# Down weights of the experts loaded as whole 16 KB rows, with the inner features interleaved to match

## The reference, cut to what matters

```
D_MODEL = 1024; N_EXPERTS = 32; D_EXPERT = 512; TOP_K_FINE = 2

def expert_block(args):
    xblk, e = args
    hid = jax.nn.silu(xblk @ w_gate[e]) * (xblk @ w_up[e])
    return hid @ w_down[e]
```

## Time and profile before

| What | Value |
|---|---|
| Time, median of 3 runs | 2542.81 us (2533.68 to 2543.42) |
| Time of the profiled execution | 2544.94 us |
| Span in its profile | 2543.2 us |
| PE matmul busy | 2271.7 us, 89% of the span |
| PE weight load busy | 1283.3 us |
| DVE, ACT, POOL busy | 825.4, 489.2, 308.4 us |
| Bytes moved by DMA | 536.48 MB |
| Loads of gate, up, down matrices | 64 each, 2048 KB each |

### The profile page before, as it was taken

The page is one execution under the profiler, slowest core; times in us unless marked ns, Lnnn a source line. Parts: engine busy times, 40 slices in busy tenths (PEclk is TensorE's granted clock), DMA queues, the critical chain, the costliest instruction groups (busy, mean ns, idle before and its releaser), DMA issues. The chain is left out here.

```text
span 2543.2 us, 33362 instructions
## 1 busy us (share of the span) xinstructions
PE 2271.7 (89%) x13415; PEld 1283.3 (50%) x13415; DVE 825.4 (32%) x1631; ACT 489.2 (19%) x894; POOL 308.4 (12%) x265
## 2 busy tenths in 40 slices
PE   6999977889958999999977999999976999999994
PEld 4687545554545445545534555554544545554541
DVE  5652125553241111111126455564323111111116
ACT  2222124341100000000013444442110010000002
POOL 5342000001101111110012000001000110110102
PEclk9999978789968999999988999999976999999997
DMA  4100010002129999999959110102108999999977
GB/s 147 35 34 1 17 68 1 1 1 71 66 100 401 420 412 405 410 412 416 415 225 301 41 37 26 30 27 61 58 25 335 417 411 409 407 405 421 400 287 282
DMA packets 144327, 536.48 MB, mean 211 GB/s; under 512 B 38370, under 2 KB 61442, under 8 KB 127792
## 3 DMA queue, kind: packets, MB, share of 16 engines
q1 hardware_dynamic: 122640, 490.93, 49.1%
q0 software_dynamic: 13600, 40.52, 4.2%
q10 hardware_dynamic: 7936, 2.90, 0.5%
HBM read 500.50 MB, written 40.50 MB: 213 GB/s over the span
## 5 line engine op out<-in xcount | busy, mean ns | idle before, releaser
L1729 PE MATMUL l_main_pgu<-l_w_ring,l_ex_xT 128*64 128x256 f32 (+1 forms) x4992 | 484.8, 383 | 2.4 <-DVE l_ex_xT L1804 1.8
L1729 PEld LDWEIGHTS l_main_pgu<-l_w_ring,l_ex_xT 128*64 128x64 f32 (+1 forms) x4992 | 292.6, 129 | 184.1 <-issue 39.7
L1775 PE MATMUL l_main_py<-l_w_ring,l_ex_hT 128*64 128x512 f32 (+1 forms) x1248 | 239.3, 595 | 1.6 <-DVE l_ex_hT L1843 1.6
L1726 PE MATMUL l_main_pgu<-l_w_ring,l_ex_xT 128*128 128x512 f32 x384 | 174.8, 610 | 15.2 <-DMA l_w_ring<-in_l_moe_w_gate 15.2
L1843 DVE COPY l_ex_hT<-l_main_ph 128x256 f32<-128x256 f32 (+1 forms) x78 | 36.3, 466 | 393.1 <-PE l_main_ph L1750 393.1
L2186 PE MATMUL lru_pr<-h2T,lru_wz 128*128 128x352 f32 (+1 forms) x480 | 144.1, 461 | 9.0 <-ACTq L2235 9.0
L1839 DVE TENSOR_TENSOR l_ex_hid<-l_ex_sil,l_main_pgu 128x256 f32<-128x256 f32 (+1 forms) x78 | 36.1, 462 | 351.2 <-PE l_main_pgu L1729 269.8
L1775 PEld LDWEIGHTS l_main_py<-l_w_ring,l_ex_hT 128*64 128x64 f32 (+1 forms) x1248 | 71.5, 128 | 136.6 <-issue 129.6
L2191 PE MATMUL lru_pg<-h2T,lru_wz 128*128 128x512 f32 x320 | 139.0, 592 | 0.0
L1726 PEld LDWEIGHTS l_main_pgu<-l_w_ring,l_ex_xT 128*128 128x128 f32 x384 | 73.2, 195 | 105.9 <-issue 87.8
L2186 PEld LDWEIGHTS lru_pr<-h2T,lru_wz 128*128 128x128 f32 x480 | 92.1, 193 | 59.4 <-ACTq L2235 9.4
(11 more groups left out here) (433 smaller groups left out, 2839.2 us busy)
## 6 DMA issues: line engine op xcount, KB each, us to landing
l_w_ring<-in_l_moe_w_gate SPq DMA_DIRECT2D x64, 2048.0 KB, 26.3
l_w_ring<-in_l_moe_w_up SPq DMA_DIRECT2D x64, 2048.0 KB, 27.4
l_w_ring<-in_l_moe_w_down SPq DMA_DIRECT2D x64, 2048.0 KB, 30.2
l_y<-expert_rows SPq DMA_DIRECT2D x32, 512.0 KB, 6.8
h_rows<-H SPq DMA_DIRECT2D x24, 512.0 KB, 5.2
lru_wz<-in_l_w_in SPq DMA_DIRECT2D x20, 512.0 KB, 4.9
H<-h_rows SPq DMA_DIRECT2D x16, 512.0 KB, 8.4
w_in<-in_l_w_in SPq DMA_DIRECT2D x3, 2048.0 KB, 8.0
```

The source lines that it names most:

```text
L1726: last = pe.matmul(out[:], x[:, k, :], w[0][:, k, :], start=k == 0, stop=k == KD - 1)
L1729: last = pe.matmul(out[HALF * h + o:HALF * h + o + m, 0:256], x[:, k, it.at + o:it.at + o + m], w[n][:, k, 256 * h:256 * h + 256], start=k ...
L1775: last = pe.matmul(py[b][HALF * h + o:HALF * h + o + m, :], hT[:, c % 2, HALF * (c // 2) + o:HALF * (c // 2) + o + m], ws[n][:, c, 512 * h ...
```

## The change

The down matrix is read as `e (p c) d -> e p (c d)`: partition p gets rows 4p to 4p+3, one piece of 16 KB. All three kinds of load now have one form. Chunk c of the down product then holds features 4p+c. To fit this,

- a big item's hidden columns are turned in steps of four (columns c, 4+c, 8+c and so on), where they were turned as a block of 128,
- in half and shared items, tile h streams of every four columns of the gate and up weights the pair 2h, 2h+1 (`half_features`), where it streamed 256 columns in a row; its hidden columns are turned in steps of two.

No instruction is added, removed or moved on any engine; the number of elements of each is the same. The products of big items (line 1726) and all down products stream what they streamed, columns in a row.

```
-    E.src["down"] = K.A[f"{L}_moe_w_down"].rearrange("e (c p) d -> e p c d", p=P)
+    E.src["down"] = K.A[f"{L}_moe_w_down"].rearrange("e (p c) d -> e p (c d)", p=P)
...
+def half_features(w, k, h):
+    return w[:, k, :].rearrange("r (p c) -> r p c", c=4)[:, :, 2 * h:2 * h + 2]
...
+def hidden_chunk(hid, c, chunks):
+    return hid[:, 0:P * chunks].rearrange("s (p c) -> s c p", c=chunks)[:, c, :]
...
 def load_unit(sp, E, unit, kind, e, sem):
-    if kind < DOWN:
-        sp.dma_start(E.ring[:, unit % UNITS, :], E.src[("gate", "up")[kind]][ds(e, 1)].rearrange("a p x -> (a p) x")).then_inc(sem, 16)
-    else:
-        sp.dma_start(down_view(E, unit), E.src["down"][ds(e, 1)].rearrange("a p c d -> (a p) c d")).then_inc(sem, 16)
+    sp.dma_start(E.ring[:, unit % UNITS, :], E.src[("gate", "up", "down")[kind]][ds(e, 1)].rearrange("a p x -> (a p) x")).then_inc(sem, 16)
...
-                            last = pe.matmul(out[HALF * h + o:HALF * h + o + m, 0:256], x[:, k, it.at + o:it.at + o + m], w[n][:, k, 256 * h:256 * h + 256],
+                            last = pe.matmul(out[HALF * h + o:HALF * h + o + m, 0:256], x[:, k, it.at + o:it.at + o + m], half_features(w[n], k, h),
...
-                for c in range(4 if items[i].big else 2):
-                    last = pe.transpose(ph[:, c, :], hid[i % 2][:, P * c:P * c + P], K.ident[:])
+                chunks = 4 if items[i].big else 2
+                for c in range(chunks):
+                    last = pe.transpose(ph[:, c, :], hidden_chunk(hid[i % 2], c, chunks), K.ident[:])
```

More of the change, by code:

```diff
@@ L1942, in step @@
                     for h in range(2):
-                        last = pe.matmul(out[HALF * h:HALF * h + HALF, 0:256], xT[par][:, k, 0:HALF], w[:, k, 256 * h:256 * h + 256], start=k == 0, stop=k == KD - 1)
+                        last = pe.matmul(out[HALF * h:HALF * h + HALF, 0:256], xT[par][:, k, 0:HALF], half_features(w, k, h), start=k == 0, stop=k == KD - 1)
                 last.then_inc(ready, 1)
@@ L1946, in step @@
             for c in range(2):
-                last = pe.transpose(ph[:, c, :], hid[par][:, P * c:P * c + P], K.ident[:])
+                last = pe.transpose(ph[:, c, :], hidden_chunk(hid[par], c, 2), K.ident[:])
             last.then_inc(self.h_turned, 1)
```

## The result

| | Before | After |
|---|---|---|
| Time, median (lowest to highest) | 2542.75 us (2533.68 to 2543.42, and one of 5448.15) | 2551.96 us (2547.39 to 2562.84) |
| Runs | 9 | 9 |
| Ratio, 95% interval | | 1.0041 [1.0026, 1.0056] |
| Profiled execution, its span | 2544.94, 2543.2 us | 2547.39, 2545.6 us |

A forecast was written before the change was run, and what follows sets the result against it. The prediction took PE to bound the kernel, but for 15.1 us of waits for gate weights. Its terms, 0 for pairs, 0 for the rest and -7.6 us for loads, took the median 2542.8 to 2535 us, range 2526 to 2600.

The forecast's parts named there:

- What bounds the kernel: Expert stages: PE sets the time, except for 15.1 us in which it waits for big items' gate weights.
- all waits, 15.1: Upper bound of faster weight loads: all PE waits for gate weights, 15.1 us; as a rival 2528 us, chance 0.1.
- The loads' term: Down matrix loads: 0.2 us saved per unit, shortening PE's waits by 3.6 us in layer 0 and 4.0 in layer 1, 7.6 us.
- The pairs' term: Gate and up products of half and shared items: pairs cost 0, at most 106 ns a slot, 224 us.
- the rival of slow pairs: Tile products: pairs lengthen every slot by 53 ns, 2640 us; decides from 13 ns a slot; chance 0.2.
- The signs given for being wrong: Line 1729's busy time above 257 us a layer with weight waits at zero, or one of its forms longer alone.
- The turns: Transposes of hidden rows in steps of 8 or 16 bytes: 78 groups cost 0, at most 4.1 us.
- Cover: Added PE time from a worse reading of the weights is hidden only by the same 15 us of waits.
- Gathers and SP: Gathers may land 3.6 us later but PE waits for none after the first; SP waits no more; cost 0.
- within 0.5%: Whole kernel: time neither faster nor slower by over 0.5%, chance 0.6; faster 0.1, slower 0.3.
- 0 + 0 - 7.6: Sum of the terms for the whole kernel: pairs 0, the rest 0, loads 7.6 us saved, giving 2535 us.
- The likely cases' own range: Whole kernel time if only the likely cases were counted: 2526 to 2548 us.

The follow-up runs named there:

- half of each down unit: Kernel before with down units loaded by whole rows, from unit 10 of each layer only half of each: 2523.08 us against 2542.41, ratio 0.992.
- The load alone: Kernel before with only the down loads changed to one 16 KB piece per partition, products and turns as before: 2537.2 us against 2540.64, ratio 0.9987.
- the 8 KB version: Kernel before with down loads in two 8 KB pieces per partition, tiles streaming columns in a row, VectorE reordering hidden columns: 2538.1 us against 2540.64, ratio 0.9993.
- the two with runs: Kernel before with tiles reading two runs of 128 columns (2573 us), or four columns of every eight (no time given); 216 ns a slot in both.
- the pairs and the turns alone: Kernel before with only the column pairs in tile products (2554.54 us, ratio 1.006), or only hidden rows turned in steps of two or four (2543.67 us, 1.0008).
- every second column: Kernel before with tile h reading every second column, even or odd: 227 ns a slot, tile products 508.2 us; no total time given.
- pairs apart: Kernel before with pairs as in the change, but tile 1 reading four k blocks away from tile 0: 2587 us, 227 ns a slot.

## Why the prediction was wrong, point by point

**What bounds the kernel: right.** PE set the time but for the stops, and the stages moved as PE's work and the stops did. One thing was left out: the stop's price. The term "all waits, 15.1" should have been about 20, as half of each down unit showed, since behind the longer stops the clock fell to half for a few us. The row was there to be read: line 1726's product took 8.83 us behind the stop and the mean of its group was 610 ns, where most other products of 512 columns stood at 592 to 595.

**The loads' term: right per unit, too large in sum.** 0.2 us a unit was measured as 0.24. The 7.6 us rested on "while the stream is full, a unit lands earlier by the saving of all down units before it". The load alone gave 3.4 us. The third stop of layer 0 went as that sentence said, but the first two there gave 0.3 us instead of 1.8, and the third of layer 1 didn't shrink at all, where 2.19 had been expected. Which part of the sentence fails is open: the ring empties at unit 41 in layer 0, but that was the layer whose third stop went, and single stops vary by 1 to 3 us between profiles of the same work. The count of early units did not forecast single stops of 2 to 5 us.

**The pairs' term: this step turned the sign.** It said 0, "by the pace" of the transposes that read one element in 32 bytes. That pace, 111 to 124 ns for 128 elements, is of the stationary operand. For the moving operand one element per line takes 451 ns for 256, twice the time, and two per line take 227 against 216. The inference from one operand to the other was not allowed, and the prediction named this gap ("the trace has no moving operand of this kind") and chose as if it were closed. The measured 11 ns a slot lay inside its bounds of 0 and 106, and under its 13 ns from which the rival of slow pairs would decide. So neither the forecast nor that rival came true, but the middle between them, which had no case of its own and so no chance. The signs given for being wrong show the same: the products' busy time was 254.5 us a layer, more than the 243 of the forecast and less than the 257 of the slow pairs, while the waits were near zero, as for the slow pairs.

**The turns: bound nearly right, value wrong.** 4.5 us against a bound of 4.1 and a choice of 0. In groups of two one longer load shows; the pace was read where eight transposes follow each other.

**Cover: right, and too small by the slow starts.** Of the 15.9 us of waits in the whole span 14.5 went, and 5.1 of slower products with them: 19.6 us of cover against 28.0 of added work. Without it the change would have cost 28 us.

**The two rules.** By the Trainium skill's rule on the least piece for line rate (DMA: Bandwidth & Descriptors, Specifications, 512 B) the loads would have gained nothing; 16 KB pieces took 0.24 us or 5% less per unit than 4 KB pieces, so here the trace disagrees by a little, as the prediction held. By its rule on lines (SBUF — State Buffer, in the part on the DMA port swizzle) the pairs would be free; they are 5% slower.

**Gathers and SP: right.** PE waited for no gather after the first of a layer.

**The range** took the time in, 2552 in 2526 to 2600, and "within 0.5%" with its 0.6 is what came. That was luck: the prediction came to a small difference by 0 + 0 - 7.6, and the measured one is small because 28 us of added work met 20 us of cover. The likely cases' own range, 2526 to 2548, missed it.

## What to carry to other kernels

Before a saving on the DMA side is paid for with anything on a busy engine, count what can be gained at all: here 20 us of stops, and of these the faster loads gave 3. Don't count on a single stop: its size differed by up to 3 us between profiles of the same work. Keep the moving operand in full 16-byte lines (runs of four float32 were as good as a row), and put a reordering on an engine with idle time, as the 8 KB version does on VectorE: it keeps the gain of the load and adds nothing to PE, though 2.5 us is too little to tell from nothing here. A price read off one operand of an instruction needn't hold for the other.

## What the runs showed of the hardware that was not expected

- A float32 matmul that reads its moving operand in runs of four elements or more takes 216 ns for 256 columns (a slot, see above), with two adjacent of every four elements, or every second one, 227 ns, with one of every four 451 ns. This fits a limit of about 1.75 ns for each 16-byte line that it opens, beside the one of the columns. It doesn't depend on whether two or four column tiles run, nor, for pairs, on whether they read the same lines.
- The stationary operand, read at one element per 32 bytes, keeps up where eight transposes follow each other: 111 ns from one to the next. Its load takes 193 ns instead of 140, and 205 ns in steps of 8 or 16 bytes; in the groups of two such transposes one longer load shows, 56 ns.
- In nine kernels (the one before, the two with runs, the load, the pairs and the turns alone, the 8 KB version, every second column, pairs apart) PE made 24 stops of 2 us or more before the product of a big item. After 20 of them this product took 8.6 to 9.9 us instead of 7.13, with a mean granted clock of 0.71 to 0.83 in it; after four (2.3, 2.3, 2.6 and 3.2 us) it took 7.13 at 1.00, and so it did after all the shorter stops.
- A unit of 2 MB takes 0.24 us less of the DMA engines in pieces of 16 KB than in pieces of 4 KB.
